# A down projection of seven block products for eight in 12 of its 44 groups

## What is computed

```python
SEQ, D_MODEL, D_FF = 256, 2048, 5632
...
        h = rmsnorm_2(x, ffn_norm[l])
        g = causal_dwconv(jnp.einsum('bsd,df->bsf', h, w_gate[l]), conv_w[l], conv_b[l])
        u = jnp.einsum('bsd,df->bsf', h, w_up[l])
        x = x + jnp.einsum('bsf,fd->bsd', jax.nn.silu(g) * u, w_down[l])
    return rmsnorm_2(x, final_norm)
```

## Time and profile before

| | us |
|---|---|
| median of 3 runs | 1992.75 (1992.71 to 1992.94) |
| the profiled execution | 1992.6 |
| its span, first to last instruction | 1990.8 |
| TensorE busy | 1981.3, 10,204 matmuls |
| VectorE busy | 1550.9 |
| ScalarE busy | 1068.0 |
| GpSimd busy | 406.4 |

### The profile page before, as it was taken

One profiled execution on the slowest core, in us unless ns is written; L12 is line 12 of the kernel. 1 busy time (PEld: TensorE's weight loads), 2 busy tenths in 40 slices (PEclk: granted clock), 3 DMA queues, 4 the chain that ended last, 5 costly groups with the idle time before them and its releaser, 6 DMA issues.

```text
span 1990.8 us, 26922 instructions
## 1 busy us (share of the span) xinstructions
PE 1981.3 (100%) x10204; PEld 1688.5 (85%) x10204; DVE 1550.9 (78%) x2314; ACT 1068.0 (54%) x1625; POOL 406.4 (20%) x381
## 2 busy tenths in 40 slices
PE   9999999999999999999999999999999999999998
PEld 8888998888888888888788888888888888888887
DVE  6876778788798776867777678689899776989954
ACT  7754544467534654654555555455555434555544
POOL 0015543300000444430222235200000000000121
PEclk9999999999999999999999999999999999999999
DMA  9664666567655334665454445655555555555564
GB/s 357 215 199 149 191 187 200 191 206 244 222 172 173 128 118 137 190 212 190 159 169 149 148 159 190 206 190 196 192 191 190 205 196 186 194 191 192 191 204 154
DMA packets 103506, 374.80 MB, mean 188 GB/s; under 512 B 11696, under 2 KB 13136, under 8 KB 102864
## 3 DMA queue, kind: packets, MB, share of 16 engines
q1 hardware_dynamic: 103088, 372.54, 56.6%
q10 hardware_dynamic: 288, 0.52, 0.1%
HBM read 370.92 MB, written 2.10 MB: 187 GB/s over the span
## 4 chain that ended last, share of the span: by engine, by line
PE 97%; DMA 1%; DVE 1%; ACT 0%; SPq 0%; issue 0%; ACTq 0%
PE psg L599 25%; PE psg L600 13%; PE psg L684 9%; PE psg L686 9%; PE psg L685 9%; PE pss L684 4%; PE pss L686 4%; PE pss L685 4%; PE pss L716 2%; PE pss L714 2%; PE pss L715 2%; PE pst L715 2%; PE pst L714 2%; PE pst L716 2%; PE pst L871 1%; PE pst L778 1%
## 5 line engine op out<-in xcount | busy, mean ns | idle before, releaser
L1249 ACT ACTIVATE s_w<-s_stage 128x1024 fp32r<-128x1024 f32 x689 | 724.6, 1053 | 647.8 <-PE psg L600 287.3
L1906 DVE TENSOR_TENSOR s_w<-s_stage,s_w 128x1024 fp32r<-128x1024 f32 x689 | 853.0, 1240 | 271.2 <-ACT s_w L1249 266.7
L599 PE MATMUL psg<-s_rh,s_w 128*128 128x512 f32 x1216 | 427.5, 394 | 0.3 <-DVE s_w L1906 0.3
L599 PE MATMUL psg<-s_ry,s_w 128*128 128x512 f32 x1024 | 361.8, 395 | 0.0
L600 PE MATMUL psg<-s_rh,s_w 128*128 128x256 f32 x1216 | 343.0, 282 | 0.0
L600 PE MATMUL psg<-s_ry,s_w 128*128 128x256 f32 x1024 | 288.7, 282 | 0.0
L599 PEld LDWEIGHTS psg<-s_rh,s_w 128*128 128x128 f32 x1216 | 228.4, 188 | 48.3 <-issue 1.0
L684 PE MATMUL psg<-s_w,s_ry 128*128 128x512 f32 x672 | 264.2, 393 | 0.0
L686 PE MATMUL psg<-s_w,s_ry 128*128 128x512 f32 x672 | 262.0, 390 | 0.0
L685 PE MATMUL psg<-s_w,s_ry 128*128 128x512 f32 x672 | 262.0, 390 | 0.0
L600 PEld LDWEIGHTS psg<-s_rh,s_w 128*128 128x128 f32 x1216 | 230.4, 189 | 0.7
(11 more groups left out here) (442 smaller groups left out, 2900.6 us busy)
## 6 DMA issues: line engine op xcount, KB each, us to landing
s_stage<-in_wo SPq DMA_DIRECT2D x96, 512.0 KB, 3.6
s_stage<-in_wg SPq DMA_DIRECT2D x88, 512.0 KB, 3.3
s_stage<-in_wu SPq DMA_DIRECT2D x88, 512.0 KB, 3.3
s_stage<-in_wd SPq DMA_DIRECT2D x88, 512.0 KB, 3.3
s_stage<-in_ain SPq DMA_DIRECT2D x64, 512.0 KB, 3.6
s_stage<-in_wkv SPq DMA_DIRECT2D x32, 512.0 KB, 4.1
s_stage<-in_bq SPq DMA_DIRECT2D x24, 512.0 KB, 3.3
s_stage<-in_bzq SPq DMA_DIRECT2D x24, 512.0 KB, 3.3
```

The costliest lines, as they stand in the source:

```text
L599: e.matmul(o, M.WH[:, r, ws], xx, start=begin, stop=False)
L1249: e.activation(M.weights(c, 0, n, shift), M.staged(c, n), ACT.Copy).then_inc(S["wh"], 1)
L1906: e.tensor_tensor(M.weights(c, 1, n, shift), M.staged(c, n), M.weights(c, 0, n, shift), ALU.subtract).then_inc(S["wl"], 1)
```

## The change

A **group** is a pair p of hidden tiles with two column blocks (2q and 2q + 1) and both token halves: a product of a 2 x 2 block matrix (activations, 128 x 128 a block) with a 2 x 2 block matrix (weights, 128 x 512 a block). Of the 44 groups of both down projections (12 pairs by two, 10 pairs by two) twelve are computed by Strassen's method in Winograd's form, with seven block products, 21 matmuls for 24. `SEVEN` names them: in the first down projection pairs 5, 8, 10 of its first half (q = 0) and 2, 5, 8, 10 of its second, in the second one pairs 5, 7 and 1, 3, 5.

- The two column blocks of a q now run side by side: pair p of block 2q, pair p of block 2q + 1, and so on; both end together. The last pair (of the last q the last three, `LASTK`) is done block by block.
- A Strassen group's weights are two loads a and b and four split tiles: a; the sum tile `TB`; b, whose first half has been overwritten by a sum; and half of a, overwritten too (512 columns).
- GpSimd makes these sums (`weight_sums`, four operations of 128 x 512) and the sums of the activations (`half_sums`, four of 128 x 128 for each of eight pairs, and their low part, `half_low`); ScalarE rounds the latter.
- Products that go to more than one output block have banks of their own (`PSO`, `PSG`), summed over the groups of a q. In the first down projection ScalarE copies these four banks to SBUF and GpSimd folds them into the output in eight additions a q; in the second VectorE folds (eight a q) and ScalarE copies one bank.
- Two more staging slots, made of buffers that the earlier stages used (`psqrb`, `ztet`), from block m = 2 on; a fourth weight slot in the down projections; four `HH` buffers.
- Of the 64 transposes 16 move into the up blocks m = 3, 5, 7, 9; the others stand ahead of plain tiles only (`spare`). The gains `FG` now lie in `X` and are loaded when all transposes are done.
- VectorE's adds of block 2q stand one tile ahead of those of block 2q + 1 (three tiles at the very end).

```diff
+SEVEN = (((5, 8, 10), (2, 5, 8, 10)), ((5, 7), (1, 3, 5)))
+PAIRS = tuple(sorted(set(a) | set(b)) for a, b in SEVEN)
+LASTK = 3
...
+    def seven(self, hv, q, p, a, b):
+
+        c, l = len(self.units), len(self.loads)
+        self.loads += [(a, 1024), (b, 1024)]
+        t = 4 * len(self.sevens)
...
+        self.units += [("raw", l, 1024, SHIFT, 0), ("sum", l, 1024, SHIFT, t + 2), ("raw", l + 1, 1024, SHIFT, t + 3), ("half", l, 512, SHIFT, t + 4)]
+        self.left += [c + 4, c + 4]
...
+            r = min(range(NR + down), key=lambda i: last.get(i, i - NR - 1))
...
+            s = l % NS if l < self.more else min(range(NS + 2), key=lambda i: last.get(i, -1))
...
+            for p in range(both):
+                if p in SEVEN[hv][q]:
+                    self.seven(hv, q, p, w[0][p], w[1][p])
+                else:
+                    for i in range(2):
+                        self.unit(w[i][p], 1024, SHIFT)
+            for i in range(2):
+                for p in range(both, kp):
+                    self.unit(w[i][p], 1024, SHIFT)
...
+            w.wait_ge("sp_lo", HEADS + idx + 1)
+            if first:
+                vacant(("o", 1), ("g", 1))
+            r = P.ring[done[0]]
+            w.wait_ge("wl", done[0] + 1)
+            three_products(M.PSO[1][:, :], sh[0], sl[0], r, w0, first, last)
+            three_products(M.PSG[1][:, :], sh[2], sl[2], r, w1, first, last).then_inc(S["units"], 1)
...
+        if tee:
+            w.wait_ge("tee", tee)
+        if P.ring_before[c] is not None:
+            w.wait_ge("units", P.ring_before[c] + 1)
...
+            if m in (3, 5, 7, 9):
+                flip_one(0, m // 2 - 1, c)
...
+            if done[0] not in P.parts:
+                spare.tick()
+            split()
...
+        for q in range(2):
+            if hv == 0 and q == 0:
+                spare.start(later(6, flips(1, 2, 3)))
+            ends = hv and q
+            after = LASTK if ends else 1
+            units = P.count[hv, q]
+            if hv:
+                nxt_down(units - after, P.sums_end[hv, q] - P.end["wd", hv, 2 * q + 1] + units, fold(hv, q))
+            else:
+                nxt_down(units - after)
+            for t in range(2):
+                add_down(hv, 2 * q, t)
+            nxt_down(after)
...
+        e.tensor_tensor(tb[:, 0:512], b[:, 0:512], a[:, 0:512], ALU.subtract).then_inc(S["tee"], 1)
+        e.tensor_tensor(tb[:, 512:1024], b[:, 512:1024], b[:, 0:512], ALU.subtract).then_inc(S["tee"], 1)
+        w.wait_ge("tee", t + 2)
+        e.tensor_tensor(b[:, 0:512], tb[:, 512:1024], a[:, 0:512], ALU.add).then_inc(S["tee"], 1)
+        w.wait_ge("tee", t + 3)
+        w.wait_ge("wl", c + 1)
+        e.tensor_tensor(a[:, 512:1024], a[:, 512:1024], b[:, 0:512], ALU.subtract).then_inc(S["tee"], 1)
...
+    w.wait_ge("flat", 16)
+    e.dma_start(M.FG, A["fg"]).then_inc(S["l_con2"], 16)
```

More of the change, by code:

```diff
@@ L208, in step, with place @@
         self.between.tick()
+    def place(self):
+        last = {}
+        for c in range(len(self.units)):
+            down = any(a <= c < b for a, b in self.downs)
+            r = min(range(NR + down), key=lambda i: last.get(i, i - NR - 1))
+            self.ring.append(r)
+            self.ring_before.append(last.get(r))
+            last[r] = c
+        last, count = {}, {}
+        for l in range(len(self.loads)):
+            s = l % NS if l < self.more else min(range(NS + 2), key=lambda i: last.get(i, -1))
+            self.slots.append(s)
+            self.before.append(last.get(s))
+            last[s], count[s] = l, count.get(s, 0) + 1
+            self.stamp.append(16 * count[s])
     def halves(self, name, j):
@@ new lines, in plain @@
+        def plain(n, u):
+            if u == 0:
+                for t in range(2):
+                    vacant(("st"[n % 2], t))
+                    held["st"[n % 2], t] = ("added", 2 * (4 * hv + n) + t + 1)
+            w.wait_ge("wl", done[0] + 1)
+            products(n, u, P.ring[done[0]], [(kk, t) for kk in range(2) for t in range(2)]).then_inc(S["units"], 1)
+            unit()
+        kp = nk // 2
+        for q in range(2):
+            ends = hv and q
+            paired = kp - (LASTK if ends else 1)
+            for p in range(paired):
+                if p in SEVEN[hv][q]:
+                    seven(q, p)
+                else:
+                    plain(2 * q, p)
+                    plain(2 * q + 1, p)
+            for u in range(paired, kp):
+                plain(2 * q, u)
+            if not ends:
+                plain(2 * q + 1, kp - 1)
+                continue
+            c = done[0]
+            for u in range(paired, kp):
+                w.wait_ge("wl", c + u - paired + 1)
+                products(3, u, P.ring[c + u - paired], [(0, 0), (1, 0)])
+            last_columns(c)
@@ L1865, in scalar_program @@
             side.start(up_block(m) if m % 2 else gate_block(m))
-        for n in range(4):
-            nxt(DOWN[hv] // 2)
-            if hv and n == 0:
-                tables()
-            if hv and n < 3:
-                side.start(squares(n))
+        for q in range(2):
+            units = P.count[hv, q]
+            side.start(later(P.sums_end[hv, q] - P.end["wd", hv, 2 * q + 1] + units + 1, shared(hv, q)))
+            if not hv:
+                nxt(units)
+            elif q == 0:
+                nxt(10)
+                tables()
+                nxt(units - 10)
+                side.start(later(7, squares(0)))
+                side.start(later(9, squares(1)))
+            else:
+                nxt(units - LASTK)
+                side.start(squares(2))
+                nxt(LASTK)
     side.drain()
@@ new lines, in flips, with nxt_down @@
+    def flips(*blocks):
+        for n in blocks:
+            for q in range(4):
+                for r in range(4):
+                    flip_one(n, q, r)
+                    if r % 2:
+                        yield
+    spare = Side()
+    def nxt_down(n, e_=None, steps=None):
+        for i in range(n):
+            if e_ is not None and i == e_ + 1:
+                side.start(steps)
+            side.tick()
+            if done[0] not in P.parts:
+                spare.tick()
+            split()
@@ L3096, in program @@
         P = plan(A)
-        assert len(P.units) == NTOT, len(P.units)
+        assert len(P.loads) == NLOAD, len(P.loads)
         S = Sems(nc, ctx)
```

449 lines of the change are left out of this document (328 added, 121 removed).

## The result

The changed kernel takes 2001.22 us (median of 4 runs, 2001.18 to 2001.91), the kernel before 1992.81: a ratio of 1.0043 with a 95% interval of 1.0031 to 1.0056. The prediction was 1988.4 us in a range of 1985 to 1996, with a chance of 0.13 for slower. The profiled execution took 2001.2 us, its span is 1999.4, 8.6 more than before.

What follows compares the result with a forecast made beforehand. TensorE was taken to bound the kernel, busy 1981.3 of 1990.8 us. From 1992.75, less 8.16 for removed matmuls, plus 3.1 of stalls and 0.7 at the tail, came 1988.4 us, range 1985.0 to 1996.0.

Steps and rivals of the forecast that it cites:

- What bounds the kernel, and what is removed: TensorE paces everything, the down projections without gaps; twelve groups lose three matmuls each, 36 x 0.2267 = 8.16 us.
- What collides: Down projections: VectorE's splits and GpSimd's sums exclude each other, alternating in full; first half 2.4 us too much, then even, no deficit.
- From the lock to the stalls: Down projections: TensorE stalls of 2.4 + 0.7 = 3.1 us, bounds 0 to 13.
- The slower rival: At each of twelve groups the tile behind is late by one GpSimd operation, 1.1 us: 13.2, 1998.5 us; chance 0.13.
- The change of column blocks: End of first down projection's first half: adds behind later splits delay TensorE 2.0 us, only 0.7 additional to the 2.4.
- Moved transposes and sums of activations: Gate and up blocks: transposes fit VectorE's 1.98 us wait; half sums delay splits up to 0.4 us; 0 taken, 0 to 1.
- the signs named for being wrong: Gaps in gate and up blocks; sums of 2 us or more beside splits with gaps at every group; or no gap.
- The end: Tail: column block 2 ends three tiles before the end instead of ten; +0.7 us, 0.3 to 1.5.

Runs made afterwards that it cites:

- short sums: Changed kernel with the four weight sums of every group cut from 512 columns to 8, so its output is another: 1988.11 us, ratio 0.9977.
- the additional operations in the kernel before: Kernel before, plus unused GpSimd operations of one weight sum's size in the second down projection: 2010.26 us; that stage 108.98 us, before 108.96.
- the load on one buffer: Changed kernel with sums cut to 8 columns, plus four GpSimd operations per group on their own buffer: 1993.40 us behind the sums, 1995.87 ahead of each.
- fills without operands: Kernel with sums cut to 8 columns and, ahead of each, two GpSimd fills of 128 x 512 with zero: 1988.17 us.
- the load ahead of short sums: Changed kernel with sums cut to 8 columns and, ahead of each, a 128 x 512 GpSimd operation on its own buffer: 1995.87 us.
- The kernel with VectorE's sums: Changed kernel with the four weight sums of a group made by VectorE instead of GpSimd: 2005.03 us.
- the one with earlier adds: Changed kernel with VectorE's adds of both column blocks one split earlier in its order, not at the very end: 2001.53 us.

## Why the prediction was wrong, step by step

- **What bounds the kernel, and what is removed**: right. With short sums the second down projection is 105.54 us, 108.96 - 3.42; 15 x 0.2267 is 3.40.
- **What collides**: the mechanism was right, and in the first half of the first down projection also its amount. The prediction let 8.8 us of GpSimd's work fall on splits there; what the 30 splits took above 1.22 us (0.68 for a half tile) is 9.9. In the second half it had 12 us falling on splits and called it even with VectorE's idle time; 12.5 were measured. For the second down projection it named no lock; 18.1 were measured. A sum was taken at 1.15 us alone; those that met no split took 1.28 to 1.30.
- **From the lock to the stalls, the step that failed.** "So the budget is VectorE's" compared VectorE's work with the time of a whole half and took only what was over: 2.4 us, then "even", then "no deficit". TensorE stood still for 6.4, 3.2 and 5.5 us at these places (the first with 2.8 at the change of blocks, the last with 0.5), the last while VectorE had 11 us of idle time. Idle time cannot be saved up: with four slots VectorE is at most four tiles ahead. A group uses up four tiles in 4.76 us, 1.2 us a tile, and VectorE needs 2.3 for one that meets an operation. Beside plain tiles of 2.72 us operations like them cost nothing (the additional operations in the kernel before), while in and behind ten of the twelve groups TensorE stood still, and VectorE's idle time elsewhere did not help. The prediction had the deciding figure, "right behind a group the four slots allow only about 1 us of lead", and left it to a rival.
- **The slower rival** was that rival: 1.1 us at each of twelve groups, 13.2 us, 1998.5. Measured: the sums cost 13.4 us in the two stages. That this is so near to 13.2 is in part luck: in and behind the groups it was 0 to 2.0 us each, 0.96 on the mean and 11.5 in all, and the rest stood elsewhere. What was held against it, that VectorE has no transposes in the second down projection, is true and beside the point: the groups there cost 1.0 us each.
- **The change of column blocks**: 2.0 us forecast, 2.8 measured, and all but 0.7 of it counted by me as part of the 2.4, which it isn't: 3.6 us of gaps at the groups of that half came on top. The working of that deadline held no exclusion, and without it, with short sums, 2.1 us were measured.
- **Moved transposes and sums of activations**: 0 taken, with 0 to 1 as bounds; 0.93. Gaps in these blocks were one of the signs named for being wrong.
- **The end**: 0.7 forecast, 0.42.
- **The sum by these values**: 1992.8 - 8.16 + 15.66 + 0.93 + 0.42 - 0.23 (what differs ahead) - 0.02 = 2001.4, for 2001.2.

The Trainium skill's rule (SBUF — State Buffer, § Who interferes with whom), that the second to issue blocks fully, agrees with the rows of group 8. Its full price, 55 us of VectorE with every sum meeting a split, lies about as far above what was measured (37) as the 21 (8.8 and 12) on which my forecast rested lies below.

**What stays open**: the load on one buffer brought back about 6 us of the 13.4 (the fall of the clock left out), with 21 to 25 us of VectorE's time for 37. I take the rest for the same cause at a higher dose, because the dose was smaller and fills without operands cost nothing, but no run with exactly the sums' dose and nobody waiting was made, and none in which GpSimd reads the staged tiles at full length without a result that is waited for. And no version here that makes the sums in full beats the kernel before: 1988.1 us, the time with short sums, is my estimate of what a kernel would have whose sums met no split.

## What to carry to other kernels

Price a resource conflict at the place where the buffer ahead of the bound engine is emptiest, not over the stage: what counts is the time per tile that the consumer takes there, against the producer's time per tile with the conflict in it. A scheme that saves the consumer's work by giving the producers more, faster consumption included, moves the bound onto them in exactly those places. And an idle engine is no free place for work while its operations exclude a busy engine's: ask what the two share before what each has left.

## What the runs showed of the hardware that I had not expected

- GpSimd operations that only write (fills of 128 x 512, 0.53 us each) do not hold VectorE's two-operand splits up, while one that reads 8 columns waits for a split's end.
- After gaps of about 2 us (the time beyond 0.227 between two matmuls' starts) TensorE's granted clock fell to its lower level (1.2 GHz) in some executions, and not in others with the same gap. Kernel with the load ahead of short sums, then the changed kernel, both at the change of blocks (stage, busy times, clock third from the end):

```profile
1593.35:1597.80 4.45, 4.45 (x13) 3.48 (x14) 4.34 (x8) 0.00 (x0) 3.05 (x4) 0.62 0.56 203
```

```profile
1595.32:1600.00 4.68, 4.18 (x17) 3.19 (x18) 4.58 (x8) 1.54 (x2) 3.24 (x2) 1.00 0.57 200
```

In the first, 7 matmuls stood 0.43 us apart instead of 0.227 and one at either end was slowed in part, 1.6 us lost, behind a gap of 1.99; in the second the gap was 2.02 and the clock stayed at the upper level. The kernel with VectorE's sums had two such falls, behind gaps of 2.02 and 2.04 us, and the one with earlier adds had one behind gaps of 1.82 and 0.94 us in close succession; with the transposes back in the first down projection the clock stayed up behind a gap of 2.04. So a gap can cost more than its length.
